# Streaming encoder step on one core: last FFN pair by tokens, norm sums over squares added on GpSimd, two small moves around the gates

## The chip, the cores and the metric

The kernel runs on one core of a Trainium2 chip. The metric is the device time of one execution in microseconds, the median of three runs. The engines are TensorE (PE in the profile), VectorE (DVE), ScalarE (ACT), GpSimd (POOL) and SyncE (SP), which only issues transfers.

## The reference

One layer over 1024 prompt frames and 64 sample frames (1088 tokens, model width 1024, float32): a half-step FFN, a mixer, a second half-step FFN and a final norm.

```
x = x + 0.5 * ((silu(h @ w_gate) * (h @ w_up)) @ w_down)      # h = rmsnorm(x) * g, FF = 2816
z = rmsnorm(x) * g_mix @ w_in                                 # q, k, v | mLSTM q, k, v, o | gates
x = x + concat(attention(q, k, v), mlstm(...)) @ w_out        # q and k normed per head of 64
x = x + 0.5 * swiglu(rmsnorm(x) * g_ffn2)                     # the second FFN
y = x * rsqrt(mean(x * x) + 1e-6) * g_final
```

## The kernel before, in words

Activations lie with features on partitions: X is 8 tiles of 128 features by 1088 tokens. Each engine has its own program written out by hand; semaphores order them. Products are made in three passes (`three_pass`, lines 248 to 250): both operands are split into a high part in the rounded type float32r and a low rest, ACT makes the high parts and DVE or POOL the low ones.

Tokens are cut in three tiles of 364, 362 and 362 (`NTILE`) for the projections and the FFN's down products, and in four of 272 (`HT`) for the up products and the output projection. The down product of an FFN goes through 11 pairs of 128 hidden features. For each pair `pe_down` makes 3 tiles x 8 feature blocks x 2 x 3 matmuls with the weights stationary, and `dve_x` (line 1194) adds half of each result to X.

Around the change:

- **Norm before the mixer.** ACT squares half a tile (4 blocks of features) at a time (line 264, into SQH), PE sums over partitions and blocks by multiplying with a matrix of ones (`norm_sum`, line 283), ACT takes the root (line 268), DVE the reciprocal (line 288), scales (line 296), ACT rounds (line 274), DVE makes the rest (line 303). The sums of tiles 0 and 1 stand between down chains of the last pair, that of tile 2 behind the first projection chain.
- **First projection.** 21 chains `unit_chain` in the order `M1`, four banks in turn. Chains of keys and queries are normed per head of 64: ACT squares (SQC), PE sums (`head_sums`, line 2217), ACT takes the root (RSC, line 1632), DVE inverts and multiplies. DVE also splits units of weights (line 1267). At the end PE transposes the gate rows into columns (`gate_columns`, line 2225), ACT copies them (COLS), and the attention begins with its scores (line 2275), a softmax on DVE and ACT, and transposes (line 2285).
- **Start of the second FFN.** During the last output chains ACT squares quarters of X (line 737, into SQT), PE sums them (`start_sum`, line 743), ACT takes the root (line 751), DVE the reciprocal (line 755); ACT and DVE split the first weights (lines 797 and 801).
- **End.** After the last pair X is transposed back in nine blocks of tokens (line 2479), ACT squares them with a running sum (line 1850), DVE and ACT make the inverse root, DVE multiplies by it and the gain row GF (line 2193) into YO, and SP stores YO. POOL loads GF once the last pair's matmuls are done.

Of the kernel before, what the change touches and what calls it, by code (L numbers as in the profile page):

```python
# [19 lines left out]
P = 128  # L20
# [35 lines left out]
def build(nc, a, o):  # L56

    with ExitStack() as ctx:
# [101 lines left out]
        GF = place("GF", [P, D], F32, rD)  # L160
# [62 lines left out]
        st = named("st", "sq ss rs rc dg rb ht bhi blo whi wlo pm silu mul tv thi tlo")  # L223
# [81 lines left out]

        def norm_wait(engine, s, n):

            engine.wait_ge(s.lo0, n + 1)
            engine.wait_ge(s.lo1, n + 1)
# [429 lines left out]
        def start_sum(pe, n):  # L739
            for kh in range(2):  # L740
                pe.wait_ge(st.sq, 15 + 2 * n + kh + 1)
                for k in range(4):
                    mm = nc.tensor.matmul(BANK[4 + n][:, 0:HT], ONES[:, :], SQT[:, kh, k], start=(kh == 0 and k == 0), stop=(kh == 1 and k == 3))  # L743
            mm.then_inc(st.ss, 1)

# [142 lines left out]
        def start_pe_pair(pe, f):  # L888
            if f:
                start_chain(pe, f, 0, 0, 0)  # L890
                start_sum(pe, 3)
                for i in range(1, 4):
                    start_chain(pe, f, 0, 0, i)
            else:
# [233 lines left out]

        def a_raw(f, odd, start):
            return AR0 if start else AR[f][odd]  # L1130

        def down_high(act, f, p, odd, i, what, start=False):
# [12 lines left out]
            else:  # L1145
                act.wait_ge(s_.d_in1 if odd else s_.d_in0, loads)
                nc.scalar.activation(WB[which][:, 0, i], RAWD[odd][:, i], ACT.Copy).then_inc(s_.dhi, 1)

        def down_low(dve, f, p, odd, i, start=False):
# [4 lines left out]
            nc.vector.tensor_tensor(WB[which][:, 1, i], RAWD[odd][:, i], WB[which][:, 0, i].bitcast(F32), ALU.subtract).then_inc(s_.dlo, 1)  # L1154
# [6 lines left out]
        DOWN_BANK = (0, 1, 2, 3, 6, 7)  # L1161

# [110 lines left out]
        def unit_chain(pe, n, slot, bank, tiles=NTILE, k0=0, k1=KT):  # L1273
            t0, w = tiles[n]
            for k in range(k0, k1):
                mm = three_pass(bank, w, WGH[:, slot, k], WGL[:, slot, k], HH[:, k, t0:t0 + w], HL[:, k, t0:t0 + w], k == k0, k == k1 - 1)
# [35 lines left out]
        def _(sp):  # L1312
# [85 lines left out]
            for b in range(NB + 1):  # L1398
# [1110 lines left out]
```

## Time and profile before

| | |
|---|---|
| median of 3 runs | 2059.22 us (2057.47 to 2061.34) |
| profiled execution, its own time | 2060.87 us |
| its span | 2059.0 us |
| granted TensorE clock, mean of the span | 0.993 |
| PE busy | 2022.5 us (98%) |
| DVE, ACT, POOL busy | 57%, 34%, 35% |

Busy time is the share in which an engine has an instruction under way; PE's matmuls overlap, so the spacing of their starts is their cost. A plain float32 matmul leaves two records.

### The profile page before, as it was taken

To read this page: it belongs to the slowest core of one execution; us is meant where nothing else is said; L and a number is where in the kernel's file an instruction comes from. 1 tells how busy PE (TensorE), PEld (TensorE's weight loads), DVE (VectorE), ACT (ScalarE), POOL (GpSimd) and SP (SyncE) were. 2 spreads that over 40 slices of the span, in tenths; PEclk is the share of its full clock that TensorE was granted. 3 is DMA by queue.
4 is the path that set the end of the run, shared out by engine and by line. 5 is a ranking of instruction groups with operands and counts; after the bars stand their busy time and mean duration, and the time that the engine had idled before them with its cause. 6 is when DMAs were issued, how large, how long until landed. Compare 5 with 4: busy or idle time off the path is not lost.

```text
span 2059.0 us, 38383 instructions
## 1 busy us (share of the span) xinstructions
PE 2022.5 (98%) x14285; PEld 1978.0 (96%) x14285; DVE 1165.6 (57%) x2016; ACT 691.8 (34%) x1371; POOL 711.6 (35%) x732
## 2 busy tenths in 40 slices
PE   7999999999999999999999999999999999999996
PEld 7999999999999999989998999999999999999996
DVE  6755444454666666754445654664454544666665
ACT  6333333333111133733335542433333333311112
POOL 2265655554211110131222430046555555411110
PEclk8999999999999999999999999999999999999999
DMA  8122221215422120342331733212112122632202
GB/s 256 43 84 74 87 68 62 88 68 210 156 91 84 42 74 4 99 121 88 99 101 59 209 85 107 74 64 95 62 62 94 62 94 84 235 102 102 91 0 98
DMA packets 151956, 194.62 MB, mean 95 GB/s; under 512 B 11448, under 2 KB 117464, under 8 KB 151872
## 3 DMA queue, kind: packets, MB, share of 16 engines
q1 hardware_dynamic: 144176, 173.85, 25.8%
q0 software_dynamic: 7696, 19.63, 3.0%
q8 instruction: 55, 0.90, 0.2%
q14 instruction: 29, 0.24, 0.0%
HBM read 142.43 MB, written 50.96 MB: 94 GB/s over the span
## 4 chain that ended last, share of the span: by engine, by line
PE 91%; issue 3%; DVE 2%; ACT 2%; DMA 1%; POOL 0%; SPq 0%; DVEq 0%; ACTq 0%; POOLq 0%
PE bank L248 28%; PE bank L250 28%; PE bank L249 28%; PE bank L2275 1%; PE bank L2294 1%; PE bank L2285 1%; PE bank L743 1%; PE bank L283 1%; DVE YO L2193 1%; DMA XIN<-in_x_prompt 1%; DVE RSC L1892 0%; PE bank L2383 0%; PE bank L2375 0%; PE bank L2385 0%; PE bank L2344 0%
## 5 line engine op out<-in xcount | busy, mean ns | idle before, releaser
L1194 DVE SCALAR_TENSOR_TENSOR X<-bank,X 128x362 f32<-128x362 f32 (+1 forms) x528 | 275.1, 533 | 191.0 <-PE bank L250 191.0
L248 PE MATMUL bank<-HH,WGH 128*128 128x362 f32 (+2 forms) x808 | 264.1, 327 | 0.0
L249 PE MATMUL bank<-HL,WGH 128*128 128x362 f32 (+2 forms) x808 | 255.2, 316 | 0.0
L250 PE MATMUL bank<-HH,WGL 128*128 128x362 f32 (+2 forms) x808 | 255.1, 316 | 0.0
L248 PE MATMUL bank<-FC,WR 128*128 128x272 f32 x768 | 223.3, 291 | 2.2 <-ACT X L693 2.0
L250 PE MATMUL bank<-FC,WR 128*128 128x272 f32 x768 | 222.7, 290 | 0.0
L249 PE MATMUL bank<-FC,WR 128*128 128x272 f32 x768 | 221.9, 289 | 0.0
L589 DVE TENSOR_TENSOR PV<-bank,PV 128x272 f32<-128x272 f32 x280 | 122.5, 439 | 148.0 <-PE bank L250 107.9
L656 POOL TENSOR_TENSOR SA<-SA,PV 128x272 f32<-128x272 f32 x160 | 136.5, 874 | 112.8 <-DVE PV L589 109.7
L248 PEld LDWEIGHTS bank<-HH,WGH 128*128 128x128 f32 x808 | 152.8, 189 | 14.7 <-issue 13.0
L469 DVE TENSOR_TENSOR WR<-RAWU,WR 128x512 fp32r<-128x512 f32 x100 | 86.4, 864 | 131.6 <-ACT WR L464 131.6
L248 PE MATMUL bank<-ABe,WBe 128*128 128x362 f32 (+1 forms) x480 | 158.0, 329 | 0.0
L248 PE MATMUL bank<-ABo,WBo 128*128 128x362 f32 (+1 forms) x480 | 157.6, 328 | 0.0
L250 PE MATMUL bank<-ABo,WBo 128*128 128x362 f32 (+1 forms) x480 | 157.1, 327 | 0.0
L250 PE MATMUL bank<-ABe,WBe 128*128 128x362 f32 (+1 forms) x480 | 157.0, 327 | 0.0
L249 PE MATMUL bank<-ABo,WBo 128*128 128x362 f32 (+1 forms) x480 | 157.0, 327 | 0.0
L249 PE MATMUL bank<-ABe,WBe 128*128 128x362 f32 (+1 forms) x480 | 156.9, 327 | 0.0
L249 PEld LDWEIGHTS bank<-HL,WGH 128*128 128x128 f32 x808 | 152.7, 189 | 1.6
L250 PEld LDWEIGHTS bank<-HH,WGL 128*128 128x128 f32 x808 | 152.6, 189 | 0.0
L248 PEld LDWEIGHTS bank<-FC,WR 128*128 128x128 f32 x768 | 145.2, 189 | 3.1 <-issue 2.2
L249 PEld LDWEIGHTS bank<-FC,WR 128*128 128x128 f32 x768 | 145.6, 190 | 0.0
L250 PEld LDWEIGHTS bank<-FC,WR 128*128 128x128 f32 x768 | 145.5, 189 | 0.0
(350 smaller groups left out, 5564.1 us busy)
## 6 DMA issues: line engine op xcount, KB each, us to landing
asp<-SA SPq DMA_DIRECT2D x44, 544.0 KB, 3.1
AR<-asp SPq DMA_DIRECT2D x22, 1088.0 KB, 5.0
RAWG<-in_w_gate SPq DMA_DIRECT2D x22, 1024.0 KB, 5.9
RAWU<-in_w_up SPq DMA_DIRECT2D x22, 1024.0 KB, 5.2
RAWDe<-in_w_down SPq DMA_DIRECT2D x12, 1024.0 KB, 4.9
RAW<-in_w_in SPq DMA_DIRECT2D x22, 512.0 KB, 3.6
RAWDo<-in_w_down SPq DMA_DIRECT2D x10, 1024.0 KB, 5.1
xsp<-X SPq DMA_DIRECT2D x8, 1088.0 KB, 6.1
```

Of the source, the lines that this page charges most:

```text
L248: nc.tensor.matmul(bank[:, 0:w], w_hi, rhs_hi, start=first, stop=False)
L249: nc.tensor.matmul(bank[:, 0:w], w_hi, rhs_lo, start=False, stop=False)
L250: return nc.tensor.matmul(bank[:, 0:w], w_lo, rhs_hi, start=False, stop=last)
L283: mm = nc.tensor.matmul(BANK[NORM_BANK[n]][:, 0:w], ONES[:, :], SQH[:, k, t0:t0 + w], start=(k == 0), stop=(k == KT - 1))
L469: nc.vector.tensor_tensor(WR[:, o, 1], weight(o, q0, mat), WR[:, o, 0].bitcast(F32), ALU.subtract).then_inc(s_.lo, 1)
L589: nc.vector.tensor_tensor(out, bank, add, ALU.add).then_inc(s_.ev, 1)
L656: nc.gpsimd.tensor_tensor(gated(j, slot), gated(j, slot), PV[j][:, tile], ALU.mult).then_inc(s_.mul, 1)
L743: mm = nc.tensor.matmul(BANK[4 + n][:, 0:HT], ONES[:, :], SQT[:, kh, k], start=(kh == 0 and k == 0), stop=(kh == 1 and k == 3))
L1194: nc.vector.scalar_tensor_tensor(out=x, in0=BANK[DOWN_BANK[i % 6]][:, 0:w], scalar=0.5, in1=x, op0=ALU.mult, op1=ALU.add).then_inc(s_.xadd, 1)
L2193: nc.vector.scalar_tensor_tensor(out=YO[0:L, b % 4, c], in0=BANK[(2 * b + half) % 8][0:L, :], scalar=f[:, 3:4], in1=GF[0:L, c], op0=ALU.mu ...
L2275: mm = nc.tensor.matmul(BANK[2 + i // 2][:, (i % 2) * 256:(i % 2) * 256 + 256], QB[rows, par, 2 * g_ + hl // 2, :], KW[rows, par, 0 if g_ ...
L2285: tr = nc.tensor.transpose(BANK[4 + w][:, i * P:(i + 1) * P], SP[:, i, w * P:(w + 1) * P], IDENT[:, :])
```

## The change

1. `norm_sum` and `start_sum` get their squares added up by POOL first: of the four blocks of a half, two and two are added, then one and one, in place. PE then multiplies one block per half by ones: 2 matmuls for 8. The second norm sum stands behind the last down chain instead of the sixth, the third behind the third projection chain instead of the first, the third start sum one chain later, the fourth behind the second first-FFN chain instead of the first. The first chain on each norm tile waits for the second half of the rests only at its middle.
2. The last pair of the second FFN is made by tokens. For each block of 128 tokens, in a bank pair: 4 transposes of X per half and on top of them, in the same bank, 6 matmuls with the activations stationary and 512 columns of the down weights moving. The factor 0.5 goes into the split of these weights. `dve_x` for this pair, and the separate transposes, are gone; ACT and DVE read the block's banks as before. GF lies elsewhere and is loaded once two pairs are done (and POOL's splits of all pairs). The last 64 tokens are stored in two halves.
3. The last head sum but one stands ahead of the gates' transposes, the last behind them; ACT copies the columns ahead of the last root.

```
@@ norm_sum
-            for k in range(KT):
-                if k % 4 == 0:
-                    pe.wait_ge(st.sq, 9 + 2 * n + k // 4 + 1)
-                mm = nc.tensor.matmul(BANK[NORM_BANK[n]][:, 0:w], ONES[:, :], SQH[:, k, t0:t0 + w], start=(k == 0), stop=(k == KT - 1))
+            for h in range(2):
+                pe.wait_ge(st.add, 4 * n + 2 * h + 2)
+                mm = nc.tensor.matmul(BANK[NORM_BANK[n]][:, 0:w], ONES[:, :], SQH[:, 4 * h, t0:t0 + w], start=(h == 0), stop=(h == 1))
             mm.then_inc(st.ss, 1)
+        def norm_add(pool, n, h):
+            t0, w = NTILE[n]
+            k = 4 * h
+            pool.wait_ge(st.sq, 9 + 2 * n + h + 1)
+            nc.gpsimd.tensor_tensor(SQH[:, k:k + 2, t0:t0 + w], SQH[:, k:k + 2, t0:t0 + w], SQH[:, k + 2:k + 4, t0:t0 + w], ALU.add).then_inc(st.add, 1)
+            pool.wait_ge(st.add, 4 * n + 2 * h + 1)
+            nc.gpsimd.tensor_tensor(SQH[:, k, t0:t0 + w], SQH[:, k, t0:t0 + w], SQH[:, k + 1, t0:t0 + w], ALU.add).then_inc(st.add, 1)
@@ start_sum (start_add is norm_add on SQT)
-                for k in range(4):
-                    mm = nc.tensor.matmul(BANK[4 + n][:, 0:HT], ONES[:, :], SQT[:, kh, k], start=(kh == 0 and k == 0), stop=(kh == 1 and k == 3))
+                pe.wait_ge(st.add, 12 + 4 * n + 2 * kh + 2)
+                mm = nc.tensor.matmul(BANK[4 + n][:, 0:HT], ONES[:, :], SQT[:, kh, 0], start=(kh == 0), stop=(kh == 1))
@@ new
+        TOKEN_BANK = (4, 0, 2, 6)
+        def pe_token_block(pe, b):
+            L, t0 = (P if b < NB else DEC), b * P
+            done = 264 + LAST * 24
...
+            if b < 4:
+                pe.wait_ge(s_.xadd, done - 24 + (8, 20, 22, 24)[b])
+            else:
+                pe.wait_ge(fin.y, 2 * (b - 3))
+            for half in range(2):
+                bank, c = token_bank(b, half), slice(512 * half, 512 * half + 512)
+                for k in range(4):
+                    nc.tensor.matmul(bank[0:L, k * P:(k + 1) * P], X[:, 4 * half + k, t0:t0 + L], IDENT[:, :], is_transpose=True, start=k == 0, stop=False)
+                for d in range(2):
+                    a_hi, a_lo = (AB[2][:, i, d, t0:t0 + L] for i in range(2))
+                    w_hi, w_lo = (WB[2][:, i, d, c] for i in range(2))
+                    nc.tensor.matmul(bank[0:L, :], a_hi, w_hi, start=False, stop=False)
+                    nc.tensor.matmul(bank[0:L, :], a_hi, w_lo, start=False, stop=False)
+                    mm = nc.tensor.matmul(bank[0:L, :], a_lo, w_hi, start=False, stop=d == 1)
+                mm.then_inc(x_tr, 1)
@@ tensor: first projection
-                unit_chain(pe, n, j % 4, BANK[c % 4])
+                unit_chain(pe, n, j % 4, BANK[c % 4], second=norm.lo1 if opens else None)
+                if c - 1 in NORMED:
+                    head_sums(c - 1)
                 if c == C1 - 1:
                     gate_columns()
-                if c - 1 in NORMED:
-                    head_sums(c - 1)
-                if c == 0:
+                if c == 2:
                     norm_sum(pe, norm, 2)
@@ tensor: start of the second FFN
-                if q in (37, 41, 45):
+                if q in (37, 41, 46):
                     start_sum(pe, (q - 37) // 4)
@@ tensor: end
-            for n in range(3):
-                pe_down(pe, 1, LAST, 0, n)
-            pe.wait_ge(s_.xadd, 2 * 264)
             for b in range(NB + 1):
...
+                pe_token_block(pe, b)
@@ scalar
-            normed_root(len(NORMED) - 1)
...
             nc.scalar.activation(COLS[0:DEC, NB:NB + 1], cols(DEC, NB, NB + 1), ACT.Copy).then_inc(g.colev, 1)
+            normed_root(len(NORMED) - 1)
@@ gpsimd
-            pool.wait_ge(s_.dmm, 2 * 264)
+            pool.wait_ge(s_.dmm, 264 + 48)
             pool.dma_start(GF[:, :], a["g_final"][0].partition_broadcast(P)).then_inc(const_in, 16)
```

In the order of instructions, first POOL between the first FFN and its stores of normed heads (the memset is the last thing it did there; `SQH` are the squares). Before:

```order
L1455 DMA out<-in_cache_k 16x512
L1456 DMA out<-in_cache_v 16x512
L1458 MEMSET RAW_58 128x1024
L1476 DMA zqk<-ZST 128x364
L1476 DMA zqk<-ZST 128x362 x2
L1478 DMA zqk<-KTT 128x1088
```

Now (two adds more of each width follow for the second and third tile):

```order
L1504 MEMSET RAW_58 128x1024
L289 TENSOR_TENSOR SQH<-SQH 128x2x364
L291 TENSOR_TENSOR SQH<-SQH 128x364
L289 TENSOR_TENSOR SQH<-SQH 128x2x364
L291 TENSOR_TENSOR SQH<-SQH 128x364
L289 TENSOR_TENSOR SQH<-SQH 128x2x362
```

Twelve adds now stand ahead of the first store.

Second, PE at the end of the first projection, from the last of the gates' transposes (`R`) over the head sums (`SQC`) to the first scores (`KW,QB`). Before:

```order
L2225 MATMUL bank<-IDENT,R_98 64x4
L2225 MATMUL bank<-IDENT,R_103 64x4
L2225 MATMUL bank<-IDENT,R_99 64x4
L2217 MATMUL bank<-SQC_106,BD 128x362 x2
L2275 MATMUL bank<-KW,QB 128x256 x4
```

Now, with the end of the last chain and the first transpose ahead:

```order
L250 MATMUL bank<-HH,WGL 128x362
L2265 MATMUL bank<-SQC_106,BD 128x362
L2273 MATMUL bank<-IDENT,R_98 128x4
...
L2273 MATMUL bank<-IDENT,R_99 64x4
L2265 MATMUL bank<-SQC_106,BD 128x362
L2324 MATMUL bank<-KW,QB 128x256 x4
```

One of the two head sums went ahead of the 27 transposes.

Third, PE at the end of the program. Before, the last matmuls of the down product and then all transposes:

```order
L250 MATMUL bank<-ABe,WBe 128x362
L248 MATMUL bank<-ABe,WBe 128x362
L249 MATMUL bank<-ABe,WBe 128x362
L250 MATMUL bank<-ABe,WBe 128x362
L2479 MATMUL bank<-IDENT,X 128x128 x64
L2479 MATMUL bank<-IDENT,X 64x128 x8
```

Now, from the end of the tenth pair into the first half block:

```order
L250 MATMUL bank<-ABo,WBo 128x362
L1197 MATMUL bank<-IDENT,X 128x128 x4
L1201 MATMUL bank<-WBe,ABe 128x512
L1202 MATMUL bank<-WBe,ABe 128x512
L1203 MATMUL bank<-WBe,ABe 128x512
L1201 MATMUL bank<-WBe,ABe 128x512
L1202 MATMUL bank<-WBe,ABe 128x512
L1203 MATMUL bank<-WBe,ABe 128x512
```

The transposes now open each half block, and the last pair's matmuls have 512 columns.

## Rows read from the trace of the kernel before

**Rows 1.** The page: span, and busy time of PE.
```profile
span 2059.0 us, 38383 instructions
...
PE 2022.5 (98%) x14285; PEld 1978.0 (96%) x14285; DVE 1165.6 (57%) x2016; ACT 691.8 (34%) x1371; POOL 711.6 (35%) x732
```

**Rows 2.** Waits of PE: total us, times, longest.
```profile
PE bank L2217 <- ACT RSC L1632: 3.7, 3, 1.6
```

**Rows 3.** Chain of waits: start, us, what; a sum of either kind.
```profile
756.12 4.89 PE bank L283 x16
...
1254.33 3.67 PE bank L743 x16
```

**Rows 4.** POOL by form: shapes, count, busy us, mean ns.
```profile
L1159 POOL TENSOR_TENSOR ABe<-AR,ABe 128x1088 fp32r<-128x1088 f32 x20 | 50.4, 2543 | 176.6 <-ACT ABe L1144 176.6
...
L631 POOL TENSOR_TENSOR PV<-PV 128x272 f32<-128x272 f32 x40 | 31.2, 779 | 0.0
```

**Rows 5.** Timeline (start, us, ...) at 203 us, and line 469 (min/median/max ns).
```profile
203.40 0.77 POOL L656 TENSOR_TENSOR SA<-SA,PV 128x272 f32<-128x272 f32 x1 [2.01 <-DVE PV L589]
...
203.51 1.21 DVE L469 TENSOR_TENSOR WR<-RAWG,WR 128x512 fp32r<-128x512 f32 x1 [0.19 <-ACT WR L464]
...
L469 DVE TENSOR_TENSOR WR<-RAWG,WR x100: 684/755/1308, 68.9 to 1729.7; 128x512 fp32r<-128x512 f32 x100
```

**Rows 6.** Timelines of ACT, DVE and POOL in the norm stage.
```profile
751.79 1.42 ACT L264 ACTIVATE SQH<-X 128x1456 f32<-128x1456 f32 x1 [2.58 <-DVE X L1194]
...
753.69 1.22 DVE L1267 TENSOR_TENSOR WGL<-RAW,WGH 128x1024 fp32r<-128x1024 f32 x1
...
761.64 2.43 DVE L288 RECIPROCAL SQH<-SQH 128x364 f32<-128x364 f32 x1 [4.28 <-ACT SQH L268]
...
773.56 1.66 DVE L303 TENSOR_TENSOR HL<-SQb,HH 128x1456 fp32r<-128x1456 f32 x1
...
807.04 0.58 POOL L1476 DMA_DIRECT2D zqk<-ZST  x1 [75.90 <-DVE ZST L1895]
```

**Rows 7.** Chain of waits from the gates to the first scores.
```profile
876.49 1.67 PE bank L2225 x27
...
880.58 0.86 PE bank L2217 x2
...
882.47 2.08 PE bank L2275 x8
```

**Rows 8.** Windows of PE: length, busy (count), granted clock, DMA.
```profile
878.00:880.00 2.00, 0.96 (x6) 1.00 1.11 341
888.00:890.00 2.00, 2.00 (x11) 0.80 0.38 133
```

**Rows 9.** Timelines of DVE and PE at the first softmax.
```profile
893.11 1.14 DVE L1951 TENSOR_SCALAR SP<-SP,DEN 128x256 f32<-128x256 f32 x4
...
898.49 1.03 PE L2285 MATMUL bank<-IDENT,SP 128*128 128x128 f32 x8
```

**Rows 10.** Timelines of ACT and DVE before the second FFN.
```profile
1289.89 1.14 ACT L797 ACTIVATE WR<-RAWG 128x512 fp32r<-128x512 f32 x2
...
1292.83 1.84 DVE L755 RECIPROCAL RSF<-RSF 128x272 f32<-128x272 f32 x1
```

**Rows 11.** Timeline of PE: first of 84 matmuls of the last pair, the last, transposes.
```profile
2019.07 0.33 PE L248 MATMUL bank<-ABe,WBe 128*128 128x362 f32 x1
...
2032.67 0.32 PE L250 MATMUL bank<-ABe,WBe 128*128 128x362 f32 x1
2033.62 3.71 PE L2479 MATMUL bank<-IDENT,X 128*128 128x128 f32 x32 [0.63 <-DVE X L1194]
```

**Rows 12.** Chain of waits, and timelines of ACT and DVE, at the end.
```profile
2033.30 3.96 DMA GF<-in_g_final
...
2052.49 0.58 ACT L1850 ACTIVATE JUNK<-bank 64x512 f32<-64x512 f32 x1
...
2054.26 1.40 DVE L2193 SCALAR_TENSOR_TENSOR YO<-bank,FS,GF 64x512 f32<-64x512 f32 x2
```

More of the change, by code:

```diff
@@ L159, in build @@
         YO = place("YO", [P, 4, D], F32, rHH)
-        GF = place("GF", [P, D], F32, rD)
+        GF = place("GF", [P, D], F32, rWG)
         JUNK = place("JUNK", [P, 4, 512], F32, rT)
@@ L1126, in up_pe, with by_token @@
                     pe_stage(pe, f, p, i // 2, i % 2)
+        def by_token(f, p):
+            return f == 1 and isinstance(p, int) and p == LAST
         def a_raw(f, odd, start):
@@ L1146, in down_high @@
                 act.wait_ge(s_.d_in1 if odd else s_.d_in0, loads)
-                nc.scalar.activation(WB[which][:, 0, i], RAWD[odd][:, i], ACT.Copy).then_inc(s_.dhi, 1)
+                nc.scalar.activation(WB[which][:, 0, i], RAWD[odd][:, i], ACT.Copy, scale=0.5 if by_token(f, p) else 1.0).then_inc(s_.dhi, 1)
         def down_low(dve, f, p, odd, i, start=False):
@@ L1271, in loads_until, with unit_chain @@
             return (j - 4) // 4 + 1 if j % 4 == 0 else (j - j % 4) // 4 + 1 + (j % 4 == 1)
-        def unit_chain(pe, n, slot, bank, tiles=NTILE, k0=0, k1=KT):
+        def unit_chain(pe, n, slot, bank, tiles=NTILE, k0=0, k1=KT, second=None):
             t0, w = tiles[n]
             for k in range(k0, k1):
+                if k == 4 and second is not None:
+                    pe.wait_ge(second, n + 1)
                 mm = three_pass(bank, w, WGH[:, slot, k], WGL[:, slot, k], HH[:, k, t0:t0 + w], HL[:, k, t0:t0 + w], k == k0, k == k1 - 1)
@@ L1458, in _ @@
             nc.gpsimd.memset(RAW4[:, 1, :, :], 0.0).then_inc(z.padded, 1)
+            for n in range(3):
+                for h in range(2):
+                    norm_add(pool, n, h)
             flat = lambda ap: ap.rearrange("p h d -> p (h d)")
@@ L1593, in _ @@
             pool.dma_start(o[10][0, 0].rearrange("h d -> d h"), CNS[:, :, LD]).then_inc(m_.cout, 16)
+            for n in range(4):
+                for kh in range(2):
+                    start_add(pool, n, kh)
             pool.wait_ge(m_.cout, 96)
@@ L2205, in _ @@
             pe_down(pe, 0, LAST, 0, 1, between=lambda: norm_sum(pe, norm, 0), at=4)
-            pe_down(pe, 0, LAST, 0, 2, between=lambda: norm_sum(pe, norm, 1), at=5)
+            pe_down(pe, 0, LAST, 0, 2, between=lambda: norm_sum(pe, norm, 1), at=KT - 1)
             def head_sums(c):
@@ L2242, in _ @@
             for c, (j, n) in enumerate(M1):
-                if c < 12 and c % 4 == 0:
-                    norm_wait(pe, norm, n)
+                opens = c < 12 and c % 4 == 0
+                if opens:
+                    pe.wait_ge(norm.lo0, n + 1)
                 pe.wait_ge(z.lo, j)
```

55 lines of the change are left out of this document (29 added, 26 removed).

## The prediction

> **What bounds the kernel now.** I read the page first: TensorE (PE) is busy 2022.5 us of a span of 2059.0 us [rows 1]. The table of PE's waits comes next, because in a kernel like this a change pays only if it takes work off PE or an idle stretch out of it. In the middle of the kernel PE waits for another engine mainly at the head sums, line 2217: three waits on ScalarE's (ACT's) root row, 3.7 us in all [rows 2]. The chain of waits then shows the price of each block that the diff touches, and the timelines of VectorE (DVE), ACT and GpSimd (POOL) what must be ready when PE comes earlier. A sum over squares, eight matmuls by ones in plain float32 (two records each), takes 4.89 us for a 364-token tile and 3.67 us for a 272-token one [rows 3].
>
> **Sums added on GpSimd.** Six of eight matmuls go, in three norm sums and four start sums. 4.89/8 = 0.61 us and 3.67/8 = 0.46 us each: 18 x 0.61 = 11.0 and 24 x 0.46 = 11.0 us off PE. In their place POOL runs two adds per half tile, of 728 and 364 elements (544 and 272 at the start). The trace has no add of 728; 272 elements take 0.78 us and 1088 take 2.54 us [rows 4], so 2.2 ns an element over 0.18 us: 1.8 + 1.0 us per half of a norm tile, 1.4 + 0.8 at the start.
>
> *First norm tile.* ACT's second square ends at 751.79 + 1.42 = 753.2 and the adds run to 756.1; the sum begins at 756.12 anyway [rows 3, 6]. So it is just in time, if POOL has a free way to the memory. DVE splits weights at 753.69 (1.22 us) and once more two microseconds later. Where such a DVE instruction meets a POOL add both are not served at once: at 203.40 POOL adds for 0.77 us, and a split of DVE that begins at 203.51 takes 1.21 us where the shortest of its kind take 0.68 [rows 5]. The excess of 0.5 is nearly the time to the end of the add. I charge one such 1.1 us wait of POOL behind the 1.22 us split to the first sum; the bounds are 0 and 2.3 (both splits). The Trainium skill, "SBUF — State Buffer", section "SBUF: two separate sides", says that a DVE instruction with two SBUF inputs and a GpSimd one that reads SBUF exclude each other for a whole instruction; with that rule the sum would carry the charge in full, without it none. The trace agrees with it at 203.51.
>
> *Behind that sum.* It ends 3.7 us sooner, so DVE's reciprocal starts that much sooner. From the reciprocal at 761.64 to the end of the second split at 773.56 + 1.66 DVE works without a gap, 13.6 us [rows 6]; PE has 11 chains of six matmuls (1.0 us each) and now only 1.2 us of the second sum ahead of the projection. Laid side by side: first split ready as PE arrives, second half 0.6 us late at the middle of the first chain (the new wait for it stands there). The third sum moves behind the third chain. Its root stands in ACT's queue ahead of the next evictions, and after it ACT has to split tile 2 before it evicts the fourth chain: reciprocal 2.4, two scalings of 2.1, then 1.4 for the last split, so ACT is free some 9 us after that sum. PE reaches the fourth chain's head sum after two chains and one head sum, about 8.5 us, but needs the squares, copy and root of ACT as well (1.4 us). That is a wait of 1.8 us. POOL's first store of normed heads is at 807.04 [rows 6]; the six pairs of adds are over some 20 us before it comes due and delay nothing. Net of the stage: 11.0 - 1.1 - 0.6 - 1.8 = 7.5 us.
>
> **Gates.** From 876.49 PE runs the gates' transposes (1.67 us), head sum, waits, head sum at 880.58, waits for ACT's root and column copy, and starts attention at 882.47 [rows 7]: 6.0 us. Now one head sum stands ahead of the transposes and covers nothing's wait, the other behind them with its inputs long done, and the copy no longer waits behind the root: 0.6 + 1.7 + 0.6 and about 0.7 for the hand-over, 3.6 us. Gain 2.3 us.
>
> **The clock behind the gates.** The granted clock is 1.00 at 878 to 880, but the eight matmuls at 882.47 take 2.08 us and the window 888 to 890 shows 0.80, so the lower level (half speed) ends near 888.8 [rows 7, 8]. Six microseconds at half speed cost about 2.9 us. Before the fall PE had done two head sums and thin transposes in six microseconds. Now that thin stretch is 3.6 us, and the window 878 to 880, with transposes behind it and part of a 1.6 us wait in it [rows 2], was still at the full level. I take the 2.9 us as won, at about 3 in 4.
>
> DVE limits this: its softmax for the first heads ends at 893.11 + 1.14 = 894.25, PE asks for it at 898.49 [rows 9], 4.2 us of slack. PE comes 7.5 + 2.3 + 2.9 = 12.7 us earlier, DVE's queue of head scalings only by about 7.9: a wait of 0.6 us. **Stage total: 12.1 us.**
>
> **Start sums.** 11.0 us off. What is late next: the weight splits of the second FFN. ACT does them right after the last-but-one root (1289.89 [rows 10]), which now belongs to a sum one chain later, while the chains come sooner. DVE then has split, add, reciprocal (1.84 us [rows 10]), split in its queue, and PE's first chain wants two splits: 1.8 us of wait (before: none). The last sum sits behind the second chain; its squares and adds arrive as PE does. I charge 0.3 us. **8.9 us.** If the adds take longer by as much as a DVE instruction in the way, at most 1.6 us more go.
>
> **Last pair by token.** Removed: 144 matmuls at 0.164 us (84 from the start at 2019.07 to that of the last at 2032.67) = 23.6 us, 24 additions on DVE, the gap at 2033, 72 transposes afterwards at DVE's pace. PE now begins at 2009.1 (60 such matmuls ahead of 2019.07, most of them 364 wide) with nine blocks of eight transposes (32 in 3.71 us, so 0.11 each) and twelve matmuls of 512 columns, not in this trace. Bounds: 0.164 (no dependence on width) and 0.164 x 512/362 = 0.232 us; the 272-column ones, faster in proportion, speak for the upper one [rows 11]. Per block 2.78 + 0.89 = 3.67 us, so 33.0 us: PE ends at 2042.1. ACT and DVE are hidden behind PE: from the gain row's arrival at 2037.3 to the last products at 2054.26 the old tail gets through eight blocks and its start, 2.1 us each [rows 12]. The gain row, loaded at 2033.30 for 3.96 us before DVE could start [rows 12], now comes before the last-but-one pair is done, behind GpSimd's last split, into space that nothing uses by then. The clock is full throughout the stretch. Behind PE's end: from the start of the last square at 2052.49 over root, reciprocal and products to the end of the span it is 6.5 us [rows 1, 12]; I take off 0.4 in which DVE was still at the block before and add 0.2 to begin: 6.3 us. End: 2048.4, **10.6 us** earlier. The last 64 tokens cost a whole block on PE all the same.
>
> **Sum.** 12.1 + 8.9 + 10.6 = 31.6 us. The profiled execution has a span of 2059.0 and took 2060.87 us; its time becomes 2029.3. The median of the three runs, 2059.22, lies 1.65 us below that execution, so the median becomes **2027.6 us**.
>
> **Rivals.**
> *The clock still falls behind the gates* (chance 0.2): 2.9 us are lost and DVE's 0.6 us wait goes, 2029.9 us. For it: there are still 1.7 us of thin transposes between two short matmul pairs.
> *The adds take twice as long* (0.12), since POOL and DVE meet far more often: the first sum then waits 4.3 us, and the wait passes to all behind it; with the others about 9 us in all, 2036 us. For it: single adds of 272 elements stretched beyond 0.78 us; against it: DVE reads one operand from the accumulator banks in most of the stretch.
> *The half clock in the token blocks* (0.04). The old tail's transposes ran at 0.11 us each [rows 11], at the full level; if the blocks counted as thin, 33 us of PE would become some 60: 2055 us. The Trainium skill, "TensorE: Matmul & The Clock Gate", Part 4 (PE-mode transpose), says that transposes do not count as activity in the way that matmuls do; by that rule alone the blocks would be at risk and the time 2055 us. The row at 2033.62 shows full speed through 32 of them, so the trace does not bear the rule out.
> *Slower than before* (0.02): the swap of operands makes the 512-column matmuls run like the plain float32 ones, 0.61 us for 364 columns [rows 3], 0.86 us each: 108 x 0.63 = 68 us more, 2096 us. It decides from 0.53 us a matmul (31.6/108 above 0.232). Against it: both operands are still written in the rounded type.
> *The change moves nothing on PE's path* (under 0.01) would need every sum hidden; PE's idle time is too small for that.
>
> **How the numbers follow.** 0.61 for the forecast. If all new waits stay out, 2023.5 to 2025; with the cold clock and half of the doubled adds, 2034. Range 2023.5 to 2034. A measurement here tells 0.2%, 4 us, from nothing; all but the last cases are far beyond it: faster 0.96, same 0.01, slower 0.03.
>
> **What would show it.** Norm sums of 1.2 us and start sums of 0.9 us on PE; POOL adds near 1.8 and 1.0 us; short PE waits for POOL or DVE at the first sum and first chain, for ACT's root at the fourth head sum, and for DVE's weight split at the start of the second FFN; granted clock 1.00 from 870 to 880; blocks of 3.6 us with no idle time; 6 us behind PE's last matmul. The prediction is wrong if the 512-column matmuls are far from 0.23 us or if a sum waits for POOL by more than 2 us.

## The result

The changed kernel takes 2034.07 us (median of 4 runs, 2031.38 to 2035.74), the kernel before 2059.31 (4 runs, 2057.47 to 2061.34): ratio 0.9876, 95% interval 0.9859 to 0.9893, so 25.2 us or 1.2% faster. The forecast was 2027.6 in a range of 2023.5 to 2034.0, whose end the median passes by 0.07 us. The profiled executions have spans of 2032.0 and 2059.0 us, 27.0 apart. Of that, 1.4 us is there before PE reaches anything that was changed: the first norm sum starts at 754.52 us, before at 755.95, behind the same matmuls. That is a difference between two executions.

The page of the kernel after: span, busy time, granted clock in 40 slices.

```profile
span 2032.0 us, 38145 instructions
...
PE 1998.2 (98%) x14165; PEld 1954.1 (96%) x14165; DVE 1165.5 (57%) x1992; ACT 692.7 (34%) x1371; POOL 752.2 (37%) x760
...
PEclk8999999999999999999999999999999999999999
```

PE has 24.3 us less to do than in [rows 1], POOL 40 us more. PE's waits after (us in total, times, longest):

```profile
PE bank L2265 <- ACT RSC L1684: 3.7, 3, 1.5
PE bank L248 <- DVE WR L809: 3.5, 2, 1.9
PE bank L248 <- ACT ZST L1763: 2.9, 1, 2.9
PE bank L248 <- DVE HL L310: 2.9, 2, 1.5
```

L2265 is the head sums' line of [rows 2]. Three kinds of wait are new: one of the two on the weight split WR (1.5 us, at the start of the second FFN), the two on VectorE's low halves HL at the first projection chain, and 2.9 us on ACT's eviction ZST, its copy of a finished chain out of an accumulator bank. The prediction has nothing of the last.

Split at four places of the two traces, the 27.0 us are as follows. The places are the first norm sum, the first transposes of attention, the first start sum and the start of the last pair; all numbers are us:

| stretch | before | after | gain |
|---|---|---|---|
| up to the first norm sum | 755.95 | 754.52 | 1.4 |
| to the first transposes, at 898.49 and 891.40 | 142.5 | 136.9 | 5.7 |
| to the first start sum, at 1254.16 and 1247.51 | 355.7 | 356.1 | -0.4 |
| to the start of the last pair, at 2009.08 and 1993.29 | 754.9 | 745.8 | 9.1 |
| to the end | 49.9 | 38.7 | 11.2 |

**Where GpSimd and VectorE meet.** Timeline of PE, DVE and POOL behind the first sum (start, us, engine, line, x how many, idle before and releaser):

```profile
754.52 0.77 PE L282 MATMUL bank<-SQH,ONES 128*128 128x364 f32 x2
...
755.56 0.88 PE L282 MATMUL bank<-SQH,ONES 128*128 128x364 f32 x2 [0.27 <-POOL SQH L291]
...
758.43 1.75 POOL L289 TENSOR_TENSOR SQH<-SQH 128x724 f32<-128x724 f32 x1 [2.92 <-ACT SQH L264]
...
760.69 3.97 DVE L303 SCALAR_TENSOR_TENSOR SQa<-X,GC,SQH 128x364 f32<-128x364 f32 x4
...
762.30 1.95 POOL L289 TENSOR_TENSOR SQH<-SQH 128x724 f32<-128x724 f32 x1 [1.07 <-ACT SQH L264]
...
765.47 2.11 DVE L303 SCALAR_TENSOR_TENSOR SQb<-X,GC,SQH 128x364 f32<-128x364 f32 x4
...
770.41 1.76 POOL L289 TENSOR_TENSOR SQH<-SQH 128x724 f32<-128x724 f32 x1 [4.92 <-ACT SQH L264]
...
770.85 2.85 DVE L310 TENSOR_TENSOR HL<-SQb,HH 128x1456 fp32r<-128x1456 f32 x1
...
772.24 2.28 POOL L291 TENSOR_TENSOR SQH<-SQH 128x362 f32<-128x362 f32 x1
...
773.75 0.43 PE L248 MATMUL bank<-HH,WGH 128*128 128x364 f32 x1 [1.39 <-DVE HL L310]
```

The first sum waits 0.27 us for POOL. But four scalings that take 2.11 us with no add beside them (at 765.47) take 3.97 at 760.69. The split that takes 1.66 us by itself [rows 6] meets the add at 770.41 and takes 2.85: it ends 1.53 us behind that add's end at 772.17, as if it had stood still until then. POOL's small add, 0.97 us by itself, takes 2.28 beside it.

**The start of attention.** PE, DVE and ACT from the gates to the first transposes:

```profile
872.25 0.85 PE L2265 MATMUL bank<-SQC,BD 128*128 128x362 f32 x2
...
873.56 1.14 PE L2324 MATMUL bank<-KW,QB 64*128 64x256 f32 x8 [0.46 <-DMA VW<-vtok]
...
879.68 0.54 DVE L1947 TENSOR_TENSOR ZST<-ZST,RSC 128x362 f32<-128x362 f32 x1
...
881.57 1.22 DVE L1988 TENSOR_REDUCE NMX<-SP 128x4 f32<-128x1024 f32 x1
...
883.22 0.51 ACT L1748 ACTIVATE SP<-SP,NMX 128x256 f32<-128x256 f32 x1 [8.22 <-DVE ESK L1994]
...
885.30 0.81 ACT L1763 ACTIVATE ZST<-bank 128x364 f32<-128x364 f32 x2
...
885.80 0.58 PE L248 MATMUL bank<-HH,WGH 128*128 128x362 f32 x1 [2.95 <-ACT ZST L1763]
...
891.40 0.82 PE L2334 MATMUL bank<-IDENT,SP 128*128 128x128 f32 x6
```

The scores take 1.14 us and not 2.08 [rows 7], at full clock. But PE does the first two mLSTM chains behind them and then stands for 2.95 us: the third chain needs the bank that ACT evicts at 885.30, and in ACT's queue the exponentials of the first softmax stand ahead of that eviction. ACT is idle 8.2 us until DVE has the softmax's row maximum, and DVE comes to that only behind its last head scaling (which ends at 880.2, before at 887.5). Then the clock falls. PE's windows (us, busy, matmuls, granted clock, DMA share, GB/s):

```profile
878.00:882.00 4.00, 4.00 (x26) 1.00 0.81 217
882.00:886.00 4.00, 1.05 (x7) 0.99 0.10 36
886.00:890.00 4.00, 4.00 (x16) 0.58 0.25 93
890.00:894.00 4.00, 4.00 (x30) 1.00 0.07 21
```

0.58 at 886 to 890 is mostly the lower level (1.2 GHz), behind a stretch in which PE was busy for 1.05 of 4 us. Before, the lower level came at the scores and was over by 889 [rows 8]. From the scores to the transposes PE now takes 17.8 us, before 16.0.

The trace of before already had the row that matters here: ACT's eviction of the first chain, and PE's start of the third.

```profile
892.58 0.45 ACT L1711 ACTIVATE ZST<-bank 128x364 f32<-128x364 f32 x1
...
894.49 0.33 PE L248 MATMUL bank<-HH,WGH 128*128 128x362 f32 x1
```

The eviction ended 1.5 us before PE asked for its bank, where the transposes had 4.2 us of slack. In the trace after, PE comes to this place 11.6 us sooner (882.85) and the eviction 7.3 us sooner.

**The tail** (timeline of PE, then the last link on DVE):

```profile
1993.29 0.60 PE L1197 MATMUL bank<-IDENT,X 128*128 128x128 f32 x4
...
1995.12 0.60 PE L1197 MATMUL bank<-IDENT,X 128*128 128x128 f32 x4
...
2026.02 0.40 PE L1203 MATMUL bank<-WBe,ABe 128*64 128x512 f32 x1
...
2027.87 1.40 DVE L2241 SCALAR_TENSOR_TENSOR YO<-bank,FS,GF 64x512 f32<-64x512 f32 x2
```

A half block takes 1.83 us, so 3.66 a block, with 512-column matmuls 0.23 us apart (2025.56, 2025.79, 2026.02); the last matmul is done near 2026.4, 5.6 us ahead of the span's end.

### The profile page after: what moved, and what is told of

Same layout as the page of the kernel before. It is cut to its first block, busy times and chain, and to the rows that moved or that the text cites. A ratio compares the mean times of both kernels' runs of the same rounds, so it can differ in the third digit from the quotient of the medians.

```text
span 2032.0 us, 38145 instructions
## 1 busy us (share of the span) xinstructions
PE 1998.2 (98%) x14165; PEld 1954.1 (96%) x14165; DVE 1165.5 (57%) x1992; ACT 692.7 (34%) x1371; POOL 752.2 (37%) x760
## 4 chain that ended last, share of the span: by engine, by line
PE 93%; DVE 3%; ACT 1%; DMA 1%; issue 1%; SPq 0%; POOL 0%; DVEq 0%; ACTq 0%; POOLq 0%
PE bank L248 29%; PE bank L250 29%; PE bank L249 28%; PE bank L2343 1%; PE bank L2324 1%; PE bank L2334 1%; DMA XIN<-in_x_prompt 1%; DVE RSC L1944 0%; PE bank L2432 0%; PE bank L1203 0%; PE bank L1201 0%; PE bank L1202 0%; PE bank L2424 0%; DVE X L1237 0%; PE bank L1197 0%
## 5 line engine op out<-in xcount | busy, mean ns | idle before, releaser
L1237 DVE SCALAR_TENSOR_TENSOR X<-bank,X 128x362 f32<-128x362 f32 (+1 forms) x504 | 262.4, 534 | 180.2 <-PE bank L250 180.2
L248 PEld LDWEIGHTS bank<-HH,WGH 128*128 128x128 f32 x808 | 152.7, 189 | 21.4 <-issue 12.7
L517 ACT ACTIVATE SA<-SA 128x272 f32<-128x272 f32 x160 | 67.0, 429 | 227.8 <-DVE SA L591 118.6
L248 PE MATMUL bank<-ABe,WBe 128*128 128x362 f32 (+1 forms) x432 | 142.1, 329 | 0.0
L249 PE MATMUL bank<-ABe,WBe 128*128 128x362 f32 (+1 forms) x432 | 141.7, 328 | 0.0
```

The source lines that it names most:

```text
L248: nc.tensor.matmul(bank[:, 0:w], w_hi, rhs_hi, start=first, stop=False)
L249: nc.tensor.matmul(bank[:, 0:w], w_hi, rhs_lo, start=False, stop=False)
L517: nc.scalar.activation(tile, tile, ACT.Silu).then_inc(s_.silu, 1)
L1237: nc.vector.scalar_tensor_tensor(out=x, in0=BANK[DOWN_BANK[i % 6]][:, 0:w], scalar=0.5, in1=x, op0=ALU.mult, op1=ALU.add).then_inc(s_.xadd, 1)
```

## The experiments

There are three batches, each on one chip with the kernel before: e1 to e4, e5 to e8, and e9 to e11. Differences of medians hold within a batch. The runs of one kernel lie 2 to 10 us apart, so beside each median stand places in its trace, counted from the first norm sum.

### One part alone

e1_tail keeps only part 2 (tokens, gain row); e2_sums only part 1; e3_gates only part 3. Each is the changed kernel with the other parts put back as in the diff's minus lines.

> Only the last pair by tokens, with the gain row's earlier load. My theory: this part held what was forecast, since in the changed kernel PE needs 1.83 us for each half block and the end lies 38.7 us behind the last matmul of the tenth pair, where before it was 49.9 us. So 11 us less than before (2048 us), and nothing different before the tenth pair. Rival: part of what is missing was lost in the tail's neighbourhood, as the matmuls of the down stage ran a little slower in the changed kernel (0.166 us instead of 0.165 apart); then this kernel gains 9 us or less and shows the slower spacing.

Measured: 2049.69 us (2049.23 to 2051.07) beside 2061.36 of before: ratio 0.9942 (0.992 to 0.9963), 11.7 us. First token transposes at 2010.67, span 2049.4: 38.7 us, the same as in the full change. So the tail is worth what it was said to be, by itself.

> Only the sums of squares on GpSimd, with their new places. My theory: the norm stage brings about 6 us up to the first scores instead of the 7.5 forecast, as the adds stretch VectorE's scalings (3.97 and 3.54 us for four where 2.1 is the rule) and PE waits 2.9 us for the low halves; the start sums bring 9. Sum 14 to 15 us, 2045 us. Rival (the loss is all behind the first softmax): here PE and VectorE both come earlier by similar amounts, so no new wait of PE for the stores' copy on ScalarE beyond 1 us may show; if it shows 2.9 us as in the changed kernel, the head sums' order has nothing to do with it.

Measured: 2048.02 us (2045.0 to 2052.56), ratio 0.9929 (0.9906 to 0.9953), 13.3 us. That is 3 us above the 2045 that was expected. From the first norm sum to the first transposes it takes 137.0 us, in the full change 136.9, and PE has no wait on the eviction here. PE in the profiled execution of e2_sums:

```profile
1135.62 0.66 PE L2391 MATMUL bank<-IDENT,ZQ 128*128 128x128 f32 x4 [1.95 <-DMA ZQ<-zm]
```

and its windows (us, busy, matmuls, clock, DMA share, GB/s):

```profile
1136.00:1140.00 4.00, 3.35 (x20) 0.60 1.10 298
...
1208.00:1212.00 4.00, 4.00 (x17) 0.56 0.01 4
```

These are two more falls of the clock, one behind a wait for the mLSTM heads' transfer, one at 1208. From the transposes to the first start sum this execution took 362.9 us where the others of this batch took 355.9 to 357.0. So its span of 2051.0 is some 6 to 7 us longer than it would be without, and its other runs reach down to 2045.

> Only the head sums around the gates' transposes and the earlier column copy. My theory: the first scores start 2 to 2.5 us earlier and at the full clock, but ScalarE evicts the first chain of the attention only behind the exponentials, which wait for VectorE's softmax, and VectorE ends at most 0.5 us earlier. PE then stands about 3 us before the third chain, falls to half clock for a while, and of the 5.2 us (2.3 of order, 2.9 of clock) about 1 to 1.5 us are left: 2058 us. Rival (the forecast's): the slack of 4.2 us at the transposes decides, and 4.5 to 5 us are left: 2054.5 us.

Measured: 2060.91 us (10 runs, 2057.22 to 2062.95), ratio 0.9994 (0.9983 to 1.0004). That is 0.5 us, with an interval from 3.5 us faster to 0.8 slower; the 4.5 to 5 us of the rival are outside it, the expected 1 to 1.5 are not told from nothing. Yet the scores begin 8.6 us behind the last head sum under a projection chain (872.17 to 880.80), before 10.8 (871.72 to 882.47), and at full clock. The time is lost again in front of the third chain:

```profile
880.80 1.14 PE L2322 MATMUL bank<-KW,QB 64*128 64x256 f32 x8 [0.78 <-DMA VW<-vtok]
...
892.73 0.67 PE L248 MATMUL bank<-HH,WGH 128*128 128x362 f32 x1 [2.63 <-ACT ZST L1758]
...
898.22 1.03 PE L2332 MATMUL bank<-IDENT,SP 128*128 128x128 f32 x8
```

It is 142.1 us from the first norm sum to the transposes, before 142.5. The three parts alone bring 11.7, 13.3 and 0.5 us, 25.5 in all: they add up to the full change.

### The eviction ahead of the exponentials

e4_evict: the changed kernel, and

```
                 for t in range(4):
+                    if first and t == 0:
+                        evict(h, 0)
                     att_exps(h * 4 + t)
-                    evict(h, 3 * t)
+                    if not (first and t == 0):
+                        evict(h, 3 * t)
```

> The changed kernel with ScalarE's eviction of the attention's first chain put ahead of the first exponentials. My theory: the 2.95 us wait of PE before the third chain goes, and with it the half clock behind it (1.2 us); the softmax is ready at 887.0 and PE asks at 887.2 for it. First transposes 4 us earlier than in the changed kernel (at 887.5 instead of 891.4), 2030 us. Rival: the wait is VectorE's lateness and moves to the transposes; then they start at 890 or later and the time stays within 1.5 us of the changed kernel.

Measured: 2033.36 us (2031.1 to 2035.16), ratio 0.9865 (0.9841 to 0.9889). The wait is gone and none took its place. The transposes stand 134.0 us behind the first norm sum, 2.9 earlier than in the changed kernel (4 were expected), though the clock fell at the scores this time:

```profile
873.84 2.06 PE L2327 MATMUL bank<-KW,QB 64*128 64x256 f32 x8 [0.83 <-DMA VW<-vtok]
...
880.80 0.47 ACT L1763 ACTIVATE ZST<-bank 128x364 f32<-128x364 f32 x1 [7.18 <-PE bank L250]
...
888.56 1.04 PE L2337 MATMUL bank<-IDENT,SP 128*128 128x128 f32 x8
```

So it was ACT's queue, not the softmax itself, that held PE. Not all of the 2.9 us is the edit's: a second trace of the changed kernel (e11_again, below), whose clock fell at the scores too, has 135.2 us, which leaves 1.3. The median, where 2030 was expected, lies 28.0 us below before, against 25.2 in the changed kernel's own comparison, and the intervals overlap: the gain is shown in the trace, not in the total.

### The changed kernel without the gates' part

e6_nogates puts the head sum, the transposes and the last root back in their old order.

> The changed kernel with the gates' part undone: gate columns ahead of the last two head sums again, and the column copy behind the last root. Theory A (the first softmax sets the start of attention, so that what the gates give is taken back by a wait of about 3 us before the third chain): the first transposes of attention come as early as in the changed kernel, within 0.5 us, though the first scores come 3 us later and the clock falls behind the gates; there is no 2.9 us wait on ScalarE's eviction; total the same within 1 us. Theory B (the prediction's: gates 2.3 us and clock 2.9 us are won in the total): total 4 to 5 us above the changed kernel.

Measured: 2035.72 us (2033.74 to 2037.1) beside 2060.84, ratio 0.9876 (0.9861 to 0.9892). The scores start at 876.85, 3.3 us later than in the changed kernel, and take 2.08 us; there is no wait on the eviction. The transposes start at 891.61, 136.9 us behind the first norm sum, as with the gates' part (136.9, and 135.2 in e11_again). The gain over before is 25.1 us, with the gates' part 25.2. That is theory A.

### The norm's row in an accumulator bank

e5_rowpsum, the changed kernel with:

```
-            nc.vector.reciprocal(square_row(n), square_row(n)).then_inc(st.rc, 1)
+            nc.vector.reciprocal(BANK[NORM_BANK[n]][:, 0:NTILE[n][1]], square_row(n)).then_inc(st.rc, 1)
...
-        in1=square_row(n), op0=ALU.mult, op1=ALU.mult)
+        in1=BANK[NORM_BANK[n]][:, 0:w], op0=ALU.mult, op1=ALU.mult)
```

(and the waits that free these banks count the scalings).

> The changed kernel, but the norm's reciprocal writes its row to an accumulator bank in place of SBUF, so that the scalings of X read one SBUF operand and not two. Everything else, the adds on GpSimd too, is as before. Theory A (a VectorE instruction with two SBUF operands and a GpSimd add hold each other up): the groups of four scalings that took 3.97 us at 760.69 and 3.54 us at 776.94 come back to 2.1 us, so the two waits of TensorE at the first chains (2.9 us in all, for VectorE's low halves) shrink to under 1 us; the split at 752.55 (two SBUF operands still) stays at 2.15 us. TensorE is some 2 us earlier at the first scores; but the first softmax sets the time there, and VectorE is earlier by the same, so the total falls by 1.5 to 2.5 us against the changed kernel. Theory B (the scalings are slow for another reason, for example they wait for a store's buffer or the GpSimd adds slow everything that touches SBUF): 3.97 stays, the waits stay 2.9 us, no gain.

Measured: 2034.05 us (2030.05 to 2035.48), ratio 0.9862 (0.9844 to 0.988). DVE and POOL there:

```profile
761.04 2.10 DVE L303 SCALAR_TENSOR_TENSOR SQa<-X,GC,bank 128x364 f32<-128x364 f32 x4
...
762.65 1.76 POOL L289 TENSOR_TENSOR SQH<-SQH 128x724 f32<-128x724 f32 x1 [1.11 <-ACT SQH L264]
...
769.31 2.85 DVE L310 TENSOR_TENSOR HL<-SQb,HH 128x1456 fp32r<-128x1456 f32 x1
...
770.70 2.28 POOL L291 TENSOR_TENSOR SQH<-SQH 128x362 f32<-128x362 f32 x1
...
775.41 2.10 DVE L303 SCALAR_TENSOR_TENSOR SQa<-X,GC,bank 128x362 f32<-128x362 f32 x4
```

The scalings' 3.97 and 3.54 us became 2.10 beside the same adds, and POOL's add beside them went from 1.95 to 1.76; the split with two SBUF operands kept its 2.85. By themselves the scalings take the same time with either source (2.11 and 2.10), so it is the meeting that went. That is theory A. The Trainium skill, "SBUF — State Buffer", section "SBUF: two separate sides", says that a DVE instruction with two SBUF inputs and a GpSimd instruction that reads SBUF exclude each other for a whole instruction, and does not list such an instruction with only one SBUF input; both agree with these rows.

Of PE's two waits on HL (2.9 us) one is left, 1.4 (expected: under 1). PE comes to the last head sum under a chain 108.8 us behind the first norm sum, 1.9 earlier than in the changed kernel, and to the transposes 133.4 us behind it. In the total this is not told from the spread: the median is 1.7 us below that of e6_nogates, and the profiled execution had the clock fall at 1132 to 1140 behind a 2.5 us wait for ZO and took 358.3 us to the first start sum.

### The weight splits ahead of the root

e7_start: `start_weight_high(act, 1, 0)` and `(act, 1, 1)` ahead of `start_root(act, 2)`, and `start_weight_low(dve, 1, 1)` ahead of `start_reciprocal(dve, 2)`.

> The changed kernel with two weight splits of the second FFN taken ahead: ScalarE does the first two high halves ahead of root 2, and VectorE the second low half ahead of reciprocal 2. Theory A (the 1.5 us wait at the second chain of that FFN is the queue behind the late root, as predicted): the wait of TensorE on VectorE's weight halves there goes from 1.5 us to under 0.3 and the total falls by 1.2 to 1.5 us. Theory B (the split waits for the weight's transfer or for something earlier): the wait stays. A third outcome: the wait moves to sum 3 or to the second pair, which now have reciprocal 2 later by 0.7 us.

Measured: 2033.74 us (2031.8 to 2036.22), ratio 0.9868 (0.9852 to 0.9884). The 1.5 us wait on WR is gone; the fourth sum waits 0.27 us for POOL instead. From the first start sum to the matmul behind the fourth it is 40.1 us, in the changed kernel and e6_nogates 41.4: 1.2 us. Up to the last pair it is 744.9 against 745.8, so 0.9 of it arrived. In the changed kernel these rows are the queue that the prediction described:

```profile
1279.57 1.85 DVE L763 RECIPROCAL RSF<-RSF 128x272 f32<-128x272 f32 x1
...
1281.33 0.63 DVE L809 TENSOR_TENSOR WR<-RAWG,WR 128x512 fp32r<-128x512 f32 x1
...
1282.02 0.39 PE L248 MATMUL bank<-FC,WR 128*128 128x272 f32 x1 [1.51 <-DVE WR L809]
```

### The edits together, and an earlier load

e8_best is e4, e5 and e7 in one; e9_vw also issues the two loads `VW[:, 0, w_] <- vtok[0]` ahead of POOL's wait for the ninth scaled head.

> The changed kernel with three edits together: the first attention chain evicted ahead of the first exponentials, the norm's row in an accumulator bank, and the start's weight splits taken ahead. If the three waits are independent, the total is 2.8 (the wait before the third chain) + 2.0 + 1.4 = about 6 us below the changed kernel, some 33 us below the kernel before, and about 2027 us. If the first softmax is the real limit, the eviction's gain shrinks: the scores' transposes then wait for VectorE, and the total is 3 to 4 us below the changed kernel. A fall of the clock behind the gates or behind the waits on the m transfers can take 1 to 3 us from either.

Measured: 2029.27 us (5 runs, 2027.83 to 2030.35) beside 2060.84, ratio 0.9843 (0.983 to 0.9857), in the batch of e5 to e7 with 2034.05, 2035.72 and 2033.74. The transposes come 130.4 us behind the first norm sum, 6.5 earlier than in the changed kernel, and the stretch from the first start sum to the last pair takes 745.2. The expected 2027 was 2 us too low; the time lies between that and the other case, 3 to 4 us below the changed kernel. Of the 12 runs of the three others one (2030.05) lies inside its range, the rest above.

> The version with the three edits together (eviction ahead of the exponentials, norm's row in an accumulator bank, weight splits ahead), and a fourth: GpSimd issues the two loads of the values for the first attention window ahead of its wait for VectorE's scaled head, in a stretch in which it idles 2.4 us, and not behind the store of that head. Theory A (the last thing that the first scores wait for is that load; in the runs so far the wait was 0.46 to 0.79 us where the clock stayed, 0.83 and 1.05 us where it fell behind it): the wait on the values is gone, the scores start 0.5 to 0.7 us behind the last head sum or wait only for the columns, and the granted clock is 1.00 from 866 to 890. The total falls by 0.5 to 1 us against the version with three edits. Theory B (the clock falls behind the gates whatever the wait is): the scores take 2.08 us again in spite of it. Theory C: another transfer of the same set arrives as late, and the wait is then put down to it, at 0.5 to 0.7 us.

Measured: 2029.02 us (2027.43 to 2033.12) beside 2060.72, ratio 0.9851 (0.9834 to 0.9867). The wait on VW is gone (0.38 us on the columns is left), the clock stayed at 1.00 from 866 to 890, and now the softmax does set the time:

```profile
871.44 1.14 PE L2330 MATMUL bank<-KW,QB 64*128 64x256 f32 x8 [0.38 <-ACT COLS L1744]
...
885.00 1.09 PE L2340 MATMUL bank<-IDENT,SP 128*128 128x128 f32 x8 [0.26 <-DVE SP L2009]
```

(The expectation counts the 0.79 us of e7_start among the waits behind which the clock stayed. Its trace shows that it fell in the middle of the scores, which took 1.35 us there.) The transposes start again 130.4 us behind the first norm sum: the 0.5 to 1 us that was expected did not come, because PE now waits for DVE's softmax there.

### Half the adds, and the changed kernel again

e10_half leaves out POOL's add of 364 (272) elements; PE sums two blocks a half.

> The changed kernel with one add per half and not two: GpSimd adds 728 (544) elements and leaves out the add of 364 (272), and TensorE sums four squares per sum and not two. Theory A (what the sums give is 0.61 and 0.46 us for each matmul taken off TensorE, as the prediction has it): 6 matmuls of 0.61 us and 8 of 0.46 us come back, 7.3 us; the waits that the second adds caused go, at most 0.3 us at the first sum and one stretched half of VectorE (1.2 us); norm sums take 2.45 us and start sums 1.8 us; total 6 to 7 us above the changed kernel. Theory B (the adds' meeting VectorE costs most of what the last two matmuls of each sum save): total within 3 us of the changed kernel.

> The changed kernel itself once more, on the chip of the two runs beside it. Open are a wait for the m heads' transfers and the pace of the second FFN's down stage, 303 matmuls in 50 us in one trace of this kernel and 305 in others of its variants. If the pace belongs to the kernel, 303 again; if it belongs to the execution, it may be 305, and the tail then starts up to 1.4 us earlier. The wait before the third attention chain (2.9 us) and the two waits on VectorE's low halves (2.9 us in all) must be there again, and the time within 2 us of 2034.

Measured, same chip: e10_half 2038.62 us (2035.54 to 2040.92), ratio 0.9895 (0.9879 to 0.9912); e11_again 2034.80 (2031.68 to 2035.81), ratio 0.9868 (0.9852 to 0.9885). So 3.8 us lie between them, neither theory's number, and the traces tell why. The start sums took 2.00 us for 1.08 (here from the first start to the last end), and from the first of them to the end of the fourth it is 45.4 us for 41.7: the 3.7 us in full. The norm sums took 2.6 us for 1.4 (3.6 in all), but the transposes came 135.8 us behind the first norm sum, in e11_again 135.2: of PE's 3.6 us only 0.5 showed. One of the two waits on HL was gone and the other 1.0 us long, and the wait for the eviction was 0.9 us for 1.5.

e11_again is the same program as the changed kernel. Its time, its two waits on HL (2.9 us) and the 303 matmuls in 50 us of the down stage are as expected; the wait for the eviction is 1.5 us and not 2.9. Its clock did fall at the scores, behind a wait of 0.38 us:

```profile
873.84 2.09 PE L2324 MATMUL bank<-KW,QB 64*128 64x256 f32 x8 [0.38 <-DMA VW<-vtok]
...
886.17 0.43 PE L248 MATMUL bank<-HH,WGH 128*128 128x362 f32 x1 [1.54 <-ACT ZST L1763]
...
890.20 1.03 PE L2334 MATMUL bank<-IDENT,SP 128*128 128x128 f32 x8
```

The window 874 to 878 of PE shows it:

```profile
874.00:878.00 4.00, 4.00 (x17) 0.61 1.08 311
```

With the clock lost there it reached the transposes 1.7 us sooner (135.2 us from the first norm sum for 136.9) than the execution that kept it. In both, PE begins the third chain 131.2 to 131.3 us behind the first norm sum, when ACT has evicted; the slower PE only waited half as long for it. But in the one the clock fell behind the long wait and the third chain took 5.6 us, in the other it stayed and the chain took 4.0. e7_start shows the same once more. Its clock fell in the middle of the scores, the wait for the eviction was 1.1 us, and the transposes came 135.2 us behind the first norm sum too:

```profile
874.73 1.35 PE L2326 MATMUL bank<-KW,QB 64*128 64x256 f32 x8 [0.79 <-DMA VW<-vtok]
```

## Why the prediction was right, and where it was not

The sign and two of the three terms held; the gain was forecast 6.4 us too large, 31.6 us for 25.2. By its terms, with the measured values from the two traces:

- **Tail, 10.6 us:** 11.2, and 11.7 alone (e1_tail). Blocks took 3.66 us for 3.67, matmuls of 512 columns 0.23 us, at full clock. The end behind PE was 5.6 us for 6.3.
- **Start sums, 8.9 us:** 9.1. The sums take 0.92 us on the chain of waits; the wait of 1.8 us for the weight split measured 1.5, the 0.3 of the last sum did not come.
- **Norm stage, 7.5 us:** from the first norm sum to the last head sum under a chain (871.72, after 865.25) it is 115.8 us before and 110.7 after: 5.0. The first sum's wait for POOL was 0.3, not 1.1, and that of the fourth chain's head sum 1.5 for 1.8, but the waits for HL were 2.9 us, not 0.6. Idle time tells too little of what such waits cost: by the distance between the starts of the matmuls around them the four cost 0.5 + 1.9 + 1.6 + 1.7 = 5.7 us, and 11.0 - 5.7 = 5.3 is near the measured 5.0. The step that failed there is "DVE reads one operand from the accumulator banks in most of the stretch": its scalings of X read two from SBUF, met the adds and took up to twice as long. e5_rowpsum shows that and gets 1.9 us back; the other wait is behind the split that meets an add, 2.85 us for 1.66, which no run took away. The charge for the meeting was laid on the first sum alone.
- **Gates, 2.3 us:** 2.4 (10.75 us before, 8.31 after, from that head sum to the scores). Its own addends, 6.0 less 3.6, make 2.4 too.
- **The clock, 2.9 us, and DVE's wait of 0.6:** of the nine traces with the gates' part the clock held at the scores in four (this one, e3, e8 and e9) and fell in five (e4, e5, e7, e10 and e11); "3 in 4" was too sure, and that it held in this trace is luck. What failed is the step behind it, "DVE limits this": I looked only at what the transposes wait for, with 4.2 us of slack, and not at what stands in ACT's queue behind the exponentials. The third chain needs ACT's eviction, and that waits with the exponentials for DVE, 5.6 us ahead of the transposes. There the slack was 1.5 us, so the forecast's own 12.7 us for PE and 7.9 for DVE would have given a wait of 3.3 us. (The 7.9 has no source in the prediction; measured, the softmax is ready 7.3 us sooner.) The cost was 2.95 us and a new fall of the clock: from scores to transposes 1.8 us more than before where 2.3 less was forecast. That swallows gates and clock both. e3_gates and e6_nogates show that the gates' part brings 0 to 1.7 us and not 5.2, alone (0.9994) or on top (136.9 and 135.2 us with it, 136.9 and 137.0 without); e4_evict shows that one moved eviction removes the wait.

So the term that was mis-sized is the 12.1 us of this stage: it measured 5.7. The other two make 19.5 by forecast and 20.3 measured. Of the rivals, "the adds take twice as long", with 2036 us nearer to the measured time than the forecast is, is partly true in its mechanism and wrong in its place: two of POOL's small adds took twice as long (1.81 and 2.28 us), the others little longer than alone, and what cost PE time was DVE's instructions. That the time lies at the range's upper end is luck in part: 2034.0 was added up from a fall of the clock at the scores and half of that rival, and what came instead were other mishaps that happen to be as large.

One reading of the prediction was too short. Against the half clock in the token blocks it set the 32 transposes at 2033.62 [rows 11], at full speed. Later in the same old tail, with PE standing still 0.94 us between groups of eight, the clock did fall: the eight at 2045.57 took 1.68 us for 1.09. The token blocks, with matmuls among the transposes and no gaps, kept it.

Open is a smaller thing: the second FFN's down stage runs 303 matmuls in 50 us in the traces of after, e3, e4, e5, e9, e10 and e11 and 305 in those of before, e1, e2, e6, e7 and e8 (1880 to 1930 us). Over its first ten pairs that is 239.3 us (after) for 237.9 (before). The first FFN's runs 303 in nearly all. The stage ahead of it, with the gate and up products, has two paces as well: from the matmul behind the fourth start sum to the first of the down stage it is 465.1 us in after, e2, e4 and e11 and 466.5 in e5 to e10. In after the one is quick and the other slow, so that they cancel: e6_nogates has the paces of before in both and the same 745.8 us from the first start sum to the last pair. The cause is open; no experiment moved it on purpose.

## What to carry to other kernels

When a stage is made faster, look at every engine's queue at the next place where PE depends on it, not only at the consumer that you have in mind: here an eviction that PE needed soon, queued behind work that waited for a third engine, gave the whole gain back, and one moved line removed the wait. Work moved to GpSimd has a price beyond its own time: it was paid by the VectorE instructions with two SBUF operands beside it, and for the scalings one operand in an accumulator bank ended that. GpSimd's second add per half saves TensorE one matmul. Where other engines set the time, in the norm stage, that bought 0.5 of 3.6 us; where TensorE did, at the start sums, it bought all 3.7.

## What the runs showed of the hardware

- GpSimd's adds took 1.76 us for 728 elements and 0.97 for 364 by themselves, as worked out from 1088 and 272. Beside a VectorE instruction with two SBUF operands the pair runs one after the other: 1.66 us became 2.85, 0.97 became 2.28. Four scalings took 3.97 and 3.54 us for 2.11. With one operand in an accumulator bank the scalings and the add beside them kept their time (2.10 and 1.76 us).
- At the scores the granted clock is not settled by the length of the wait just before them: in one and the same program it held behind 0.46 us and fell behind 0.38. Among the variants it held behind 0.38, 0.68 and 0.78 us (e9, e8, e3) and fell behind 0.79, 0.83, 0.97 and 1.05 (e7, e4, e10, e5). Further falls came in some executions behind waits for the mLSTM heads (e2, e5, e9) and near 1208 us (e2, e11). From the transposes to the first start sum most executions take 355.7 to 356.1 us; e2 with its two falls took 362.9, e11 359.3, e5 358.3 and e9 356.6. Such falls may be much of what lies between the runs of one kernel, but only the profiled executions show them, so that is not shown.
- Blocks of four transposes and six 512-column matmuls without gaps kept the full clock for 33 us (granted clock 1.00 from 1993 to 2026). Transposes alone, with PE busy for about half of the time, kept it from 2036 to 2045 and then lost it (0.50 at 2046 to 2048 in the trace of before).
